# Delta rule: key and query products in two row halves of the tensor array, and two levels of block doubling as diagonal blocks in two opposite corners of it

## The reference, cut to what matters

```
m = jnp.where(strict, jnp.einsum('bhncd,bhnsd->bhncs', kb, kc) * decay, 0.0)
tmat = lax.linalg.triangular_solve(m + eye, eye, left_side=True, lower=True, unit_diagonal=True)
u = tmat @ vb
w = tmat @ (kb * exp(gc))
qk = jnp.einsum('bhncd,bhnsd->bhncs', qc, kc) * decay
def step(s, inp):
    v_new = u_i - w_i @ s
    o_i = qd_i @ s + qk_i @ v_new
    s = s * gl_i + kd_i.T @ v_new
```

## Time and profile before

| | us |
|---|---|
| median of 3 runs | 3584.64 |
| lowest and highest | 3584.15, 3587.2 |
| time of the profiled execution | 3586.9 |
| its span in the trace | 3585.1 |
| TensorE busy | 3371.8 (94%) |
| VectorE, ScalarE, GpSimd busy | 1654.0, 1228.8, 1046.9 |
| mean granted clock of TensorE, share of full speed | 0.972 |

### The profile page before, as it was taken

One profiled execution on the slowest core, in us unless ns is written; L12 is line 12 of the kernel. 1 busy time (PEld: TensorE's weight loads), 2 busy tenths in 40 slices (PEclk: granted clock), 3 DMA queues, 4 the chain that ended last, 5 costly groups with the idle time before them and its releaser, 6 DMA issues.

```text
span 3585.1 us, 40898 instructions
## 1 busy us (share of the span) xinstructions
PE 3371.8 (94%) x16548; PEld 2505.5 (70%) x16548; DVE 1654.0 (46%) x3116; ACT 1228.8 (34%) x2212; POOL 1046.9 (29%) x896
## 2 busy tenths in 40 slices
PE   7999999888899999989799998999999998999998
PEld 3346888655688865645688856888887447848886
DVE  7744446498466666224456524122224117621213
ACT  2413233347323235125433314212213226733222
POOL 0233444450244420011345402222222022024443
PEclk9999999999999999999999999999999999999999
DMA  7424555210355541110111120111111111012222
GB/s 296 186 91 156 206 204 200 88 47 1 111 207 200 200 183 47 47 48 1 32 42 44 28 79 28 71 71 48 71 71 48 53 46 67 1 47 94 97 105 81
DMA packets 67613, 335.42 MB, mean 94 GB/s; under 512 B 32416, under 2 KB 35424, under 8 KB 42592
## 3 DMA queue, kind: packets, MB, share of 16 engines
q1 hardware_dynamic: 66560, 330.56, 25.0%
q10 hardware_dynamic: 864, 2.24, 0.2%
HBM read 325.86 MB, written 6.91 MB: 93 GB/s over the span
## 4 chain that ended last, share of the span: by engine, by line
PE 80%; DVE 10%; ACT 4%; DMA 2%; POOL 2%; issue 2%; SPq 1%; POOLq 0%; DVEq 0%; ACTq 0%
PE PSB L556 17%; PE PSB L648 14%; PE PSB L652 14%; PE PSB L649 14%; PE PSB L1234 3%; PE PSB L1256 2%; PE PSB L1243 2%; PE PSB L2982 1%; DVE SB L389 1%; DMA SB<-in_ada 1%; PE PSB L1795 1%; DVE SB L1328 1%; PE PSB L2419 1%; DVE SB L1639 1%; DVE SB L1637 1%
## 5 line engine op out<-in xcount | busy, mean ns | idle before, releaser
L652 PE MATMUL PSB<-R,WSR 128*128 128x512 f32 x2556 | 871.7, 371 | 0.0
L556 PE MATMUL PSB<-SB 128*128 128x512 f32 x1760 | 655.1, 534 | 11.6 <-ACT SB L1454 9.4
L622 POOL TENSOR_TENSOR WSR<-SB,ahead 128x1024 fp32r<-128x1024 f32 x164 | 393.0, 2397 | 674.1 <-ACT ahead L591 674.1
L556 PEld LDWEIGHTS PSB<-SB 128*128 128x128 f32 x1760 | 338.8, 193 | 325.2 <-issue 298.9
L648 PE MATMUL PSB<-R,ahead 128*128 128x512 f32 x1528 | 561.9, 368 | 0.0
L649 PE MATMUL PSB<-R,ahead 128*128 128x512 f32 x1528 | 546.0, 367 | 0.0
L652 PEld LDWEIGHTS PSB<-R,WSR 128*128 128x128 f32 x2556 | 449.3, 189 | 63.8
L622 POOL TENSOR_TENSOR WSR<-SB,ffn_weights 128x1024 fp32r<-128x1024 f32 x96 | 230.1, 2397 | 390.2 <-ACT ffn_weights L591 390.2
L648 PE MATMUL PSB<-R,ffn_weights 128*128 128x512 f32 x868 | 324.9, 374 | 8.1 <-POOL WSR L622 8.1
L648 PEld LDWEIGHTS PSB<-R,ahead 128*128 128x128 f32 x1528 | 286.9, 188 | 62.9
L649 PEld LDWEIGHTS PSB<-R,ahead 128*128 128x128 f32 x1528 | 286.9, 188 | 48.7
(11 more groups left out here) (377 smaller groups left out, 4888.2 us busy)
## 6 DMA issues: line engine op xcount, KB each, us to landing
SB<-in_w SPq DMA_DIRECT2D x95, 2048.0 KB, 8.1
SB<-in_ada SPq DMA_DIRECT2D x96, 1024.0 KB, 5.1
SB<-gate_rows SPq DMA_DIRECT2D x12, 512.0 KB, 4.4
SB<-in_rpb SPq DMA_DIRECT2D x8, 448.0 KB, 3.5
spill<-SB SPq DMA_DIRECT2D x1, 3072.0 KB, 9.6
SB<-gate_rows SPq DMA_DIRECT2D x24, 128.0 KB, 3.7
SB<-spill SPq DMA_DIRECT2D x1, 3072.0 KB, 9.8
SB<-in_x SPq DMA_DIRECT2D x8, 256.0 KB, 6.3
```

The source lines that it names most:

```text
L556: ins = e.mm(banks[ring[(g + c) % len(ring)]][0:m, 0:n], t[:, 0:m], xs[k][:, lo:lo + n], k == 0, k == nkt - 1)
L622: e.tt(lr, t, hf, ALU.subtract).then_inc(*G.up(("lo", j)))
L652: ins = e.mm(b[:, 0:n], wl, xh[:, lo:lo + n], False, last)
```

## The change

Four edits in the delta rule's stage.

- Key and query products read `KT` itself, 64 partitions of it, against the same 64 partitions of the other operand. For each head pair x the matmul of y = 0 (rows 0 to 63 of the array) and that of y = 1 (rows 64 to 127) follow each other. `KZ` is no longer filled: `key_rows_act` and the two memsets are gone. The number of matmuls stays.
- Key products of y = 0 and y = 1 of chunk n + 2 stand together ahead of level 6's second product; query products of both stand together behind u.
- At levels 4 and 5 each head's two products become two of 64 by 64 with 64 columns streamed, one per diagonal block: block (0 to 63, 0 to 63), then block (64 to 127, 64 to 127). Here y counts no longer groups of heads but the two blocks, and a bank holds one block of all eight heads. TensorE waits for both y before the first matmul of each pass, and for both before the transposes.
- VectorE's `Y` and `DM` instructions work on 64 partitions with 8 by 64 elements in each, instead of 128 partitions with 4 by 128.

In the diff the semaphore increments behind each call are left out where the call is otherwise whole.

```diff
-            e.wait_ge(*st.at("key_rows", n, y))
             for x in range(4):
-                e.mm(bank(n, "kk", y)[:, col(x)], KZ[y][:, col(x)], kb(n)[:, col(x)])
+                for y in range(2):
+                    e.mm(bank(n, "kk", y)[:, col(x)], KT[x][par(y), cl], kb(n)[par(y), col(x)])
...
-                            e.mm(bank(n, "kq", y)[:, col(x)], KZ[y][:, col(x)], QT[x][:, cl])
+                            for y in range(2):
+                                e.mm(bank(n, "kq", y)[:, col(x)], KT[x][par(y), cl], QT[x][par(y), cl])
...
                         for y in range(2):
                             free(e, n, "y", y, lv)
                             e.wait_ge(*st.at("d", n, y, lv - 1))
-                            for x in range(4):
-                                e.mm(bank(n, "y", y, lv)[:, col(x)], MT[g0 + y][:, col(x)], DM[g0 + y][:, col(x)])
+                        for h in range(8):
+                            for y in range(2):
+                                e.mm(bank(n, "y", y, lv)[par(y), col(h, 64)], g3(MTd[d])[par(y), h, par(y)], g3(DMd[d])[par(y), h, par(y)])
                         for y in range(2):
                             free(e, n, "d", y, lv)
                             e.wait_ge(*st.at("y", n, y, lv))
...
-                            for x in range(4):
-                                e.mm(bank(n, "d", y, lv)[:, col(x)], DT[g0 + y][:, col(x)], Y[g0 + y][:, col(x)])
+                        for h in range(8):
+                            for y in range(2):
+                                e.mm(bank(n, "d", y, lv)[par(y), col(h, 64)], g3(DTd[d])[par(y), h, par(y)], g3(Yd[d])[par(y), h, par(y)])
+                        for y in range(2):
+                            e.wait_ge(*st.at("d", n, y, lv))
                         for y in range(2):
                             free(e, n, "t", y, lv)
-                            e.wait_ge(*st.at("d", n, y, lv))
...
-                    kk(n + 2, 0)
+                    kk(n + 2)
...
-                    kk(n + 2, 1)
...
-                    kq(n + 2, 0)
+                    kq(n + 2)
...
-                    kq(n + 2, 1)
...
-                            v.tt(g3(Y[g0 + y]), g3(bank(n, "y", y, lv)), rep(K[("lvF", "lvB")[d]][:, col(lv)]), ALU.mult)
+                            v.tt(g3(Yd[d])[par(y), :, par(y)], h3(bank(n, "y", y, lv)[par(y), :]),
+                                 K[("lvF", "lvB")[d]][par(y), lv * 128 + 64 * y:lv * 128 + 64 * y + 64].unsqueeze(1).broadcast_to([64, 8, 64]),
+                                 ALU.mult)
...
-                            v.tt(DM[g0 + y], DM[g0 + y], bank(n, "d", y, lv), ALU.subtract)
+                            t = g3(DMd[d])[par(y), :, par(y)]
+                            v.tt(t, t, h3(bank(n, "d", y, lv)[par(y), :]), ALU.subtract)
```

More of the change, by code:

```diff
@@ L2215, in gdn @@
             AT = tiles(2, 1024)
-            Y = tiles(4, 512)
+            Yd = tiles(2, 1024)
+            Y = [Yd[d][:, y * 512:(y + 1) * 512] for d in range(2) for y in range(2)]
             BLK, INV = ([RX[par(d), i * 256:(i + 1) * 256] for d in range(2)] for i in range(2))
@@ L2265, in gdn @@
                 use(n, "o")
-                use_front(n + 2, ("kq", 1), ("tok", 1))
+                use_front(n + 2, ("tok", 1))
             use("out", 3), use("out", 0)
@@ L2344, in inverse_sp, with kk_pe @@
                     e.load(g3(DTd[d])[col(b, 16), :, col(b, 16)], inverses[d, :, b].rearrange("m r c -> r m c")).then_inc(inverse_in[d], 16)
-            def kk_pe(e, n, y):
-                free(e, n, "kk", y)
+            def kk_pe(e, n):
+                d, c, cl, j0 = chunk(n)
+                for y in range(2):
+                    free(e, n, "kk", y)
                 e.wait_ge(*st.at("key_beta", n))
-                e.wait_ge(*st.at("key_rows", n, y))
                 for x in range(4):
-                    e.mm(bank(n, "kk", y)[:, col(x)], KZ[y][:, col(x)], kb(n)[:, col(x)]).then_inc(*P.up(("kk", n, y)))
+                    for y in range(2):
+                        e.mm(bank(n, "kk", y)[:, col(x)], KT[x][par(y), cl], kb(n)[par(y), col(x)]).then_inc(*P.up(("kk", n, y)))
             def front_pe(e, i):
@@ L2357, in front_pe, with kk, kq @@
                         e.wait_ge(*mst.at("score_read", 42 + y))
-                        kk_pe(e, 0, y)
+                    kk_pe(e, 0)
             def pe(e):
                 e.wait_ge(later_landed, 16)
-                def kk(n, y):
+                def kk(n):
                     if n < 12:
-                        kk_pe(e, n, y)
-                def kq(n, y):
+                        kk_pe(e, n)
+                def kq(n):
                     if n < 12:
                         d, c, cl, j0 = chunk(n)
-                        free(e, n, "kq", y)
+                        for y in range(2):
+                            free(e, n, "kq", y)
                         for x in range(4):
-                            e.mm(bank(n, "kq", y)[:, col(x)], KZ[y][:, col(x)], QT[x][:, cl]).then_inc(*P.up(("kq", n, y)))
+                            for y in range(2):
+                                e.mm(bank(n, "kq", y)[:, col(x)], KT[x][par(y), cl], QT[x][par(y), cl]).then_inc(*P.up(("kq", n, y)))
                 def tokens(n, i):
@@ L2388, in pe @@
                     if n:
-                        kk(n, 0), kk(n, 1)
-                    kq(n, 0), tokens(n, 0), kq(n, 1), tokens(n, 1)
+                        kk(n)
+                    kq(n), tokens(n, 0), tokens(n, 1)
                 for n in range(12):
@@ L2417, in pe @@
                                 e.wait_ge(*st.at("dt", n, y, lv - 1))
-                            for x in range(4):
-                                e.mm(bank(n, "d", y, lv)[:, col(x)], DT[g0 + y][:, col(x)], Y[g0 + y][:, col(x)]).then_inc(*P.up(("dy", n, y, lv)))
+                        for h in range(8):
+                            for y in range(2):
+                                e.mm(bank(n, "d", y, lv)[par(y), col(h, 64)], g3(DTd[d])[par(y), h, par(y)], g3(Yd[d])[par(y), h, par(y)]).then_inc(
+                                    *P.up(("dy", n, y, lv)))
+                        for y in range(2):
+                            e.wait_ge(*st.at("d", n, y, lv))
                         for y in range(2):
                             free(e, n, "t", y, lv)
-                            e.wait_ge(*st.at("d", n, y, lv))
                             for x in range(4):
@@ L2472, in decay_act @@
                     e.act(t, t, ACT.Exp, bias=NG[:, j:j + 1]).then_inc(*A.up(("decay", n, y)))
[L2474 to L2481, removed]
             def front_act(e, i):
-                if i == 41:
-                    key_rows_act(e, 0)
-                elif 43 <= i < 47:
+                if 43 <= i < 47:
                     decay_act(e, (i - 43) // 2, (i - 43) % 2)
@@ L2734, in front_pool @@
             def front_pool(e, i):
[L2735 to L2740, removed]
+                if i == 53:
                     inverse_pool(e, 0)
```

22 lines of the change are left out of this document (8 added, 14 removed).

## The result

The changed kernel takes 3723.69 us (median of 4 runs, 3720.34 to 3727.81), the kernel before 3585.64 (4 runs, 3584.15 to 3587.2). The ratio is 1.0383, with a 95% interval of 1.0369 to 1.0396: slower by 138 us. The forecast was 3611, with a range that ended at 3645. The direction was right; the loss was five times the 26 us forecast.

The account below looks back on a forecast made before the run. TensorE's ring (25.05 us a chunk) and a transfer ring (25.15) were taken to bound the delta rule. +11 us at full clock and 15 for clock falls made +26: 3613 profiled, 3611 as median, range 3591 to 3645.

Parts of the forecast that it names:

- Passes in two corners: Levels 4 and 5: 32 records of 64 by 64 in opposite corners overlap, 1.0 us a pass instead of 1.8.
- The VectorE pair: Levels 4 and 5: two VectorE instructions one after the other, 1.46 us, with TensorE waiting for both.
- A level: Level 4 or 5 takes 6.4 us where it was 5.33 and 5.37, +1.05 us each.
- Level 6 with the key products: Level 6 and key products in row halves: 3.7 us against 4.23, -0.5 us a chunk.
- The whole ring: TensorE's work per delta-rule chunk: net +1.2 us, 26.25 us, now slower than the transfers' 25.15 us.
- The term of +11 us: Delta rule at full clock: +0.9 us on each of 11 turns, 9.9, and +1 for chunk 0's two levels.
- Rival B: Corners or row halves don't overlap: 45 to 67 us in 12 chunks on top of rival A, 3640 to 3660; 11%.
- Rival D: TensorE's freed time counts in full, the transfer ring decides at 25.15 us a turn: 3581; 7%.
- rival A: TensorE's clock does not fall in the delta rule: only +11 us, 3596; 20%.
- The 0.15 us for a change of tile: TensorE's change of tiling mode costs about 0.15 us, about six more a chunk, most at waits.
- The clock: Delta rule: TensorE falls to half clock in each of 11 chunks, 1.4 us each, 15 us.
- Rival C: Clock stays down through both levels, 4 and 5: some 2 us a chunk more, 24 us, 3635; 12%.

Follow-up runs that it names:

- the run with filled waits: Changed kernel plus unneeded matmuls in its four waits for VectorE per chunk, full tiles or 64 by 64: 3615.35 and 3615.30 us, before 3589.17.
- row halves alone: Changed kernel with levels 4 and 5 as before, only key and query products in row halves: 3592.75 us, kernel before 3589.17.

## Why the prediction was wrong

*The parts at full clock: right, a little low.* Passes in two corners 1.0 us and 0.2 for the end of the last result: measured 1.15. The VectorE pair 1.46: 1.41. A level 6.4: measured 6.40 and 6.53 in the run with filled waits. Level 6 with the key products 3.7: 3.91. The stretch from u on, 8.83 less 0.9, that is 7.93: 8.25 (from 2015.17 to the next L2410 at 2023.42, 27.0 us behind 1996.46). Up to level 4, 1.77: 1.87. The whole ring was forecast at 26.25 us and measured at 27.0 with filled waits. The term of +11 us was 26 us by the runs with filled waits: some 17 in the ten steady chunks (27.2 less 25.5 us each), the rest ahead of them and behind. Rival B (no overlap) is refuted by the pair of corner records, 32 in 1.15 us, and of row halves, 16 in 1.16 us. Rival D is refuted by the VectorE pair, rival A by the clock. The 0.15 us for a change of tile counts one record too few: 16 steps of 0.061 are 0.98 of the 1.07 us, which leaves 0.09.

*The clock: the step that failed.* It said: "A fall over one level costs between half and all of its TensorE work again, 1.5 to 2.9 us; the following dense part may end it. I take 1.4 us: 15 us." That a fall comes in every chunk was right. That it lasts about one level, and that dense work ends it, was not read from any row but assumed, and 1.4 us lies under the lower of its own two bounds. Measured, the low stretches of the steady part were mostly 17 and 34 us long, over the levels, level 6, u, state and output. They cost 37.1 - 27.2 = 9.9 us a chunk (means of ten, without and with filled waits) where 1.4 stood; the filled waits show it as 108 us in all where 15 stood. Rival C came nearest to the mechanism, but let the fall end with the levels, and its 24 us were a slip even so: 5.8 us at double price less 1.4 are 4.4 us a chunk, 48 us in 11, which is outside the range.

The trace of before held a warning that I read only for the fall: in the earlier trace rows the last window has TensorE busy for 6.90 of 6.90 us at 0.51, and the first for 5.10 of 5.10 at 0.50. Both say that a busy TensorE can stay at half clock. The range should have reached to a stage that stays at half clock throughout: 11 chunks with some 20 us of TensorE work each, by my estimate 220 us more. The measured 108 is half of that. Why TensorE at unbroken work does not get the full clock back sooner stays open; no run here was made for it.

The Trainium skill, "TensorE: Matmul & The Clock Gate" (What's actually happening), has the full clock back after a short time of sustained work. By that a fall would have been cheap. Here the trace disagrees, with 13.65 us of unbroken work at half clock in the run with row halves alone, and the measurement decides. That short idle times between groups of matmuls, if frequent, make the clock swing is told in that page of the Trainium skill under "A second HAM failure mode: psum-queue depth-cycling", the section behind the one that the prediction names. Here the trace agrees, with waits of 1.55 us between passes of 1.15 us.

## What to carry to other kernels

Before TensorE's work between two dependent waits is made shorter, ask what fills the time that it frees: if nothing does, the clock may go, and then the work behind it can cost double, also what was not touched (here for up to 34.1 us). Idle time gained in a chain that alternates between TensorE and VectorE was worth nothing here. The alternation of two groups was worth more than fewer VectorE instructions: at full clock the corners took 24.0 to 25.7 us a chunk with it and 27.0 without. Whether the clock is the cause can be shown by one run with useless matmuls in the waits.

## What was not expected of the hardware

- The clock fell after 10.20 us in which TensorE was busy for 7.67, with waits of 1.55 us, and in the kernel with row halves alone 1.2 us behind an idle of 1.31 us. It held, but for 17.1 of 280.6 us, with waits of 0.87 us and TensorE at work in 2.02 of 2.9 us.
- Once low it stayed so for 13.65 us in which TensorE was busy all the time (row halves alone), and for 34.1 us in which it was busy for 28.84 (the changed kernel).
- In the waits, tiles of 64 by 64 in one corner held the clock as well as full ones: 3615.30 and 3615.35 us, low for 10.2 of 271.7 us in both.
- A VectorE instruction on 64 partitions costs what it costs on 128: two of 64 by 512 in 1.41 us, two of 128 by 512 in 1.46.
